# Working out the places of overflowing tokens inside the expert stage, and an output projection that begins with a prompt tile and ends with a sample tile in two column halves

## What is computed

```python
y = concat(gla_o, nsa_o) @ w_out                  # output projection, 1024 x 1024
x = x + gate1 * y                                  # residual; gate, scale, shift: one set for the
h2 = rmsnorm(x, g_ffn) * (1 + scale2) + shift2     # prompt, one for each sample sequence
top_logit, top_idx = top_k(h2 @ w_router + b_router, 4)   # of 32 experts
top_w = softmax(top_logit)
# tokens grouped by expert in blocks of 128 rows; for each block with its expert e:
gate = minimum(xb @ w_gate[e] + b_gate[e], 7)
up = clip(xb @ w_up[e] + b_up[e], -7, 7)
y[rows] += row_w * (((up + 1) * gate * sigmoid(1.702 * gate)) @ w_down[e] + b_down[e])
x = x + gate2 * y ; out = rmsnorm(x, g_final)
```

## Time and profile before

| | us |
|---|---|
| median of 3 runs | 1974.83 |
| lowest, highest | 1967.1, 1976.14 |
| the profiled execution: its own time | 1965.11 |
| its span, first to last instruction | 1963.4 |
| mean granted TensorE clock | 0.927 of full speed |
| TensorE, VectorE busy, of the span | 1737.5 (88%), 1436.0 (73%) |
| DMA over the span | 516.53 MB, mean 263 GB/s |

### The profile page before, as it was taken

How to read it: one execution, slowest core, us unless ns; L and a number is a source line. 1 busy time by engine, 2 the same in 40 slices (tenths; PEclk the granted TensorE clock), 3 DMA queues, 4 the chain that set the end, 5 groups by cost and what they waited for, 6 DMA issues and landing times. The chain is left out here.

```text
span 1963.4 us, 27138 instructions
## 1 busy us (share of the span) xinstructions
PE 1737.5 (88%) x9025; PEld 1347.3 (69%) x9025; DVE 1436.0 (73%) x1294; ACT 1094.1 (56%) x1031; POOL 298.8 (15%) x322
## 2 busy tenths in 40 slices
PE   4999857787775986899999999999999999999982
PEld 3767555554544445788888888888888888888872
DVE  4421164455453556799999999999999999999993
ACT  3211143444331223677777777777777777777762
POOL 0000032210010401121121211211212112121110
PEclk9999878778887986899999999999999999999996
DMA  9343264330024414899999999999999999999973
GB/s 356 129 165 133 70 191 130 125 113 1 1 66 151 156 73 181 332 362 371 368 365 378 368 370 367 367 378 361 375 376 360 380 371 370 377 367 370 379 260 114
DMA packets 112070, 516.53 MB, mean 263 GB/s; under 512 B 25853, under 2 KB 47117, under 8 KB 59242
## 3 DMA queue, kind: packets, MB, share of 16 engines
q1 hardware_dynamic: 99098, 485.77, 65.9%
q0 software_dynamic: 12912, 29.98, 5.6%
HBM read 502.69 MB, written 31.81 MB: 272 GB/s over the span
## 5 line engine op out<-in xcount | busy, mean ns | idle before, releaser
L2516 PE MATMUL banks<-split 128*128 128x512 f32 x4608 | 1081.9, 394 | 1.6 <-DVE split L2671 1.6
L2516 PEld LDWEIGHTS banks<-split 128*128 128x128 f32 x4608 | 863.4, 189 | 195.8 <-issue 14.7
L2671 DVE TENSOR_TENSOR split<-expert_buffers,split 128x2048 fp32r<-128x2048 f32 x384 | 867.5, 2285 | 63.2 <-ACT split L2606 61.2
L2606 ACT ACTIVATE split<-expert_buffers 128x2048 fp32r<-128x2048 f32 x384 | 733.3, 1918 | 251.4 <-PE banks L2516 225.4
L2454 POOL TENSOR_TENSOR expert_buffers<-routing 128x1 f32<-128x1 f32 x63 | 61.0, 968 | 912.4 <-PE banks L2523 531.0
L443 PE MATMUL banks<-w_in_high,hT_high 128*128 128x476 f32 (+1 forms) x240 | 93.4, 389 | 7.7 <-DVE hT_low L369 7.7
L382 DVE COPY arena<-banks 128x476 f32<-128x476 f32 (+1 forms) x15 | 9.8, 651 | 112.4 <-PE banks L443 112.4
L443 PE MATMUL banks<-w_in_low,hT_high 128*128 128x476 f32 (+1 forms) x240 | 91.8, 382 | 0.0
L443 PE MATMUL banks<-w_in_high,hT_low 128*128 128x476 f32 (+1 forms) x240 | 91.5, 381 | 0.0
L302 ACT ACTIVATE arena<-banks 128x476 f32<-128x476 f32 (+1 forms) x15 | 8.5, 566 | 126.6 <-PE banks L443 126.6
L2675 DVE TENSOR_TENSOR split<-banks,split 128x1024 fp32r<-128x1024 f32 x64 | 77.7, 1214 | 0.2 <-ACT split L2609 0.2
(11 more groups left out here) (347 smaller groups left out, 1721.6 us busy)
## 6 DMA issues: line engine op xcount, KB each, us to landing
expert_buffers<-in_w_gate SPq DMA_DIRECT2D x128, 1024.0 KB, 7.3
expert_buffers<-in_w_up SPq DMA_DIRECT2D x128, 1024.0 KB, 5.6
expert_buffers<-in_w_down SPq DMA_DIRECT2D x128, 1024.0 KB, 9.0
arena<-in_w_ada SPq DMA_DIRECT2D x16, 1024.0 KB, 4.8
w_in_landing<-in_w_in SPq DMA_DIRECT2D x6, 1904.0 KB, 15.0
arena<-in_w_ada SPq DMA_DIRECT2D x4, 2048.0 KB, 21.5
arena<-in_x_prompt SPq DMA_DIRECT2D x8, 512.0 KB, 10.4
arena<-in_cache_cmp POOLq DMA_DIRECT2D x32, 128.0 KB, 3.2
```

The lines of the kernel that those rows point to most:

```text
L2516: last = pe.matmul(ps[:, bank + c, :], x[:, kt * P:(kt + 1) * P].bitcast(F32R), wt.bitcast(F32R), start=False, stop=(kt == KT - 1 and x is ...
L2606: act.activation(high[:, j % RING_Q].bitcast(F32R), v, ACT.Copy).then_inc(s_high, 1)
L2671: dve.tensor_tensor(rest[:, j % RING_Q].bitcast(F32R), v, high[:, j % RING_Q], ALU.subtract).then_inc(s_rest, 1)
```

## The change

1. The nine instructions on overflowing tokens become a function `place_overflow`, which VectorE runs in the expert stage between `read_gate(0)` and the remainder of quarter 7. What it reads moves to memory that stays valid. `overflow` gets a wait on it (`s_over`).
2. `project_out(0)` starts once the first w_out half and tile 0 are there. The sample tile is turned behind it.
3. The sample tile's two matmuls for each `kt` write one bank: columns 0 to 511 to partitions 0 to 63, columns 512 to 1023 to partitions 64 to 127. ScalarE copies the upper half to partitions 0 to 63, VectorE multiplies each half by itself.
4. In the expert stage `used_blocks` moves: on SP, TensorE and ScalarE behind the first work. SP waits for one used quarter, not four, before it loads block 1's biases and weights. ScalarE rounds block 1's quarters 0 and 1 before it turns to that block's rows; VectorE takes quarter 0's remainder before reading up, quarter 1's before the activation.

```diff
@@ output_and_router, TensorE
-            for t, (t0, n) in enumerate(TILES):
+            def turn_mix(t):
+                n = TILES[t][1]
...
-            pe.wait_ge(s_mta, NT)
-            pe.wait_ge(s_mtd, NT)
+            for t in range(ST):
+                turn_mix(t)
             pe.wait_ge(s_wo, 16)
             def project_out(t):
                 t0, n = TILES[t]
+                pe.wait_ge(s_mta, t + 1)
+                pe.wait_ge(s_mtd, t + 1)
...
-                        last = pe.matmul(ps[0:n, 4 + 2 * (t % 2) + c, :], mixT[:, kt, t0:t0 + n],
-                                         wout[:, kt, c * 512:(c + 1) * 512], start=(kt == 0), stop=(kt == KT - 1))
+                        out = ps[0:n, 4 + 2 * (t % 2) + c, :] if t < ST else ps[64 * c:64 * c + 64, 4, :]
+                        last = pe.matmul(out, mixT[:, kt, t0:t0 + n], wout[:, kt, c * 512:(c + 1) * 512],
+                                         start=(kt == 0), stop=(kt == KT - 1))
...
             for t in range(NT):
                 project_out(t)
+                if t == 0:
+                    turn_mix(ST)
@@ output_and_router, ScalarE
+                if t == ST:
+                    act.wait_ge(s_yp, NT)
+                    act.activation(junk[0:n, 512:1024], ps[64:64 + n, 4, :], ACT.Copy).then_inc(s_upper, 1)
@@ output_and_router, VectorE
+                if who:
+                    dve.tensor_tensor(hh[:, 0:512], ps[0:n, 4, :], ex[0:n, who, 0, 0:512], ALU.mult)
+                    dve.wait_ge(s_upper, 1)
+                    link(dve.tensor_tensor(hh[:, 512:1024], junk[0:n, 512:1024], ex[0:n, who, 0, 512:1024], ALU.mult))
@@ experts, SP, step
-                    free = [4, 4, None]
+                    free = [1, 1, None]
@@ experts, TensorE
             turn_rows(0, first=True)
+            nb, nb1, nb2, _ = used_blocks(pe)
             gate(0, 0)
@@ experts, ScalarE
-            for j in range(1, 7):
+            for j in range(1, 6):
                 high_part(j, None)
+            nb, nb1, nb2, _ = used_blocks(act)
+            high_part(6, None)
             sigmoid(0)
             high_part(7, None)
+            for j in range(2):
+                high_part(j, 0)
             rows_T(1)
-            for j in range(4):
+            for j in range(2, 4):
                 high_part(j, 0)
@@ experts, VectorE
             read_gate(0, 4)
+            place_overflow(core, dve, linker(dve, s_dve, dve_count)).then_inc(s_over, 1)
             rest_part(7, None)
-            activations(0, 8)
+            rest_part(0, 0)
+            read_up(0, 8)
             rest_T(xh, xl, s_xh, 2, s_xt)
-            for j in range(4):
+            rest_part(1, 0)
+            activate(0)
+            for j in range(2, 4):
                 rest_part(j, 0)
```

More of the change, by code:

```diff
@@ L149, in take, with linker @@
         return self.tensor[:, at:at + words]
-def linker(engine, sem):
-    count = [0]
+def linker(engine, sem, count=None):
+    count = [0] if count is None else count
     def link(ins):
@@ L1905, in output_and_router @@
     core.tabf = late.take(NSLOT)
+    core.oh = oh = late.take(NT * TOPK * NE).rearrange("p (t j e) -> p t j e", t=NT, j=TOPK)
+    core.starts = late.take(NT * TOPK * NE).rearrange("p (t j e) -> p t j e", t=NT, j=TOPK)
+    core.wn, core.over, core.one4, core.first, core.oidx = (
+        late.take(NT * TOPK).rearrange("p (t j) -> p t j", t=NT) for _ in range(5))
+    core.ostart, core.token, core.slots = late.take(NE), late.take(NT), late.take(OVER)
+    wn, over, ostart = core.wn, core.over, core.ostart
     own.end = core.z_late
-    wt, wn = (own.take(NT * TOPK).rearrange("p (t j) -> p t j", t=NT) for _ in range(2))
+    wt = own.take(NT * TOPK).rearrange("p (t j) -> p t j", t=NT)
     wr = own.take(KT * NE).rearrange("p (k n) -> p k n", k=KT)
@@ L1919, in output_and_router @@
     nv0, wsum = own.take(NT), own.take(NT)
-    oh = own.take(NT * TOPK * NE).rearrange("p (t j e) -> p t j e", t=NT, j=TOPK)
     selb = own.take(NT * NE // 2).bitcast(BF16).rearrange("p (t e) -> p t e", t=NT)
     beforeb, onesb = own.take(P // 2).bitcast(BF16), own.take(P // 2).bitcast(BF16)
-    cnt, nover, oend, ostart, ones = (own.take(NE) for _ in range(5))
+    cnt, nover, oend, ones = (own.take(NE) for _ in range(4))
     pick = own.take(TOPK * NE).rearrange("p (j e) -> p j e", j=TOPK)
-    rank, over, one4, first, oidx = (own.take(NT * TOPK).rearrange("p (t j) -> p t j", t=NT) for _ in range(5))
+    rank = own.take(NT * TOPK).rearrange("p (t j) -> p t j", t=NT)
     low4, tok4, wt4 = (own.take(TOPK) for _ in range(3))
@@ L1931, in output_and_router @@
     at_exp = placed.take(NT * TOPK * 2 * NE).rearrange("p (t j w e) -> p t j w e", t=NT, j=TOPK, w=2)
-    starts = placed.take(NT * TOPK * NE).rearrange("p (t j e) -> p t j e", t=NT, j=TOPK)
     upper = Stack(core, core.z1 + NT * D, ARENA)
@@ L2101, in _ @@
                 project_out(t)
+                if t == 0:
+                    turn_mix(ST)
+                if t == 1:
+                    pe.wait_ge(s_mta, NT)
+                    pe.wait_ge(s_mtd, NT)
                 if t >= 1:
@@ L2164, in _ @@
             dve.tensor_copy(core.unit, core.const("one"))
-            for m in (rank, wn, oh):
+            dve.tensor_copy(core.token, core.const("token"))
+            dve.tensor_copy(core.slots, core.const("iota_k")[:, 0:OVER])
+            for m in (rank, wn, oh, over):
                 dve.memset(m, 0.0)
```

44 lines of the change are left out of this document (25 added, 19 removed).

## The result

| | before | changed |
|---|---|---|
| median, us (19 runs each) | 1970.72 | 1958.41 |
| lowest, highest | 1963.05, 1980.05 | 1951.04, 1968.27 |
| ratio, 95% interval | | 0.9935 [0.9917, 0.9953] |
| profiled execution: span, granted clock | 1963.4, 0.927 | 1959.3, 0.924 |

The change takes 12.3 us off; 1955.7 was forecast, in a range of 1946 to 1967. By the ratio it is 0.65% faster (0.47 to 0.83 by the interval), as the likeliest case had it. The steps did not come out as well as the sum.

The account below looks back on a forecast made before the run. TensorE was taken to bound the expert loop at 35.62 us a block, so the change only moves its start. 3.7 + 5.7 + 2.7 + 3.0 = 15.1 us off 1970.8 gave 1955.7, range 1946 to 1967.

Parts of the forecast that it names:

- the likeliest case: Whole kernel: faster by more than about 0.5%, chance 0.81.
- Step 1, tile 0 first: Output stage: projecting tile 0 before turning the sample tile brings tile 1's h2 3.7 us earlier.
- Step 2, the sample halves: Output stage: the sample tile's column halves run side by side, so VectorE begins that tile 5.7 us earlier.
- Step 3, the stage's end: End of output stage: without the nine overflow instructions the barrier opens 2.7 us earlier, GpSimd's drain last.
- Step 4, into the experts: First expert blocks: reordered loads and remainders gain 3.0 us, bounds a gain of 5 and a loss of 4.
- A, the port on tile 0: Output stage: GpSimd's bias split delays VectorE on tile 0; gain 13 us, time 1958, chance 0.14.
- B, halves not side by side: Sample tile's projection: still takes 14.2 us; gain 9.3 us, time 1961.5, chance 0.09.
- C: Experts' start: TensorE waits for quarter 7's remainder, the clock falls, 4 us lost; gain 8, time 1963, chance 0.07.
- D: Expert loop: another beat set by VectorE or DMA, slower; 1992 us at 1.2 us more a block, chance 0.03.

Follow-up runs that it names:

- busy_wait: The changed kernel with six more matmuls, result unused, on TensorE between tile 1's projection and turning tile 0's h2; 1957.03 us, ratio to before 0.9917.
- inputs_first: The changed kernel with prompt scales, g_ffn and tile 0's rows loaded ahead of the other tiles' rows; 1952.87 us, ratio to before 0.9922.
- no_tile0: The changed kernel with the sample tile turned before the projection starts, as before the change; 1961.54 us, ratio to before 0.9955.
- overflow_back: The changed kernel with the nine overflow instructions back at the end of the output stage; ratio to before 0.9934.
- sp_waits4: The changed kernel with SP again waiting for 4 used quarters, not 1, before loading block 1's biases; one execution, no ratio.
- gffn_early: The changed kernel with the load of g_ffn issued ahead of x, behind the router's weights; ratio to before 0.9936.

## Why the prediction came out as it did

**Step 1, tile 0 first: wrong.** Forecast 3.7 us at tile 1's h2; measured there, 2.2 us later than before (66.1, 63.9), and S is 0.4 us later (88.2, 87.8): 1.8 came back since tile 3's first half ran at full speed, a case that the forecast had named with 1.7. The start of the projection, the length of a tile and the place of the wait were as written. Two steps failed.

The first is "It was ready at 658.21 ... without the short wait for the projection it is ready at 657.9. TensorE turns it there: 5.6 us gained of 8.9, the rest turns into a wait for VectorE." VectorE was ready 42.7 us into the stage, not 40.2. g_ffn came 33.3 to 34.6 us into the stage in the five profiles with tile 0 first and the old order of loads, 29.6 to 32.1 in the four without; SP's issues of the rows, ahead of g_ffn's, took 8.3 to 8.7 us in them, not 7.1 to 8.2. Why they take longer was not tried and stays open. And the wait was priced at its length alone: behind 6.25 us of idleness TensorE's clock was 0.50 and 5.3 us of work were lost.

The second is "I leave GpSimd's start at 657". That is 39.4 into the stage; the split began at 43.2. By the forecast's own rule, VectorE is done 1.1 us behind GpSimd's second long operation, and this operation ended at 687.1, 62.8 into the stage, not 59.1. So tile 1's h2 was ready at 63.9, not at 60.2, and that alone takes all of the 3.7 us; the lower clock put TensorE another 2.2 behind it. busy_wait shows both: with the wait filled, h2(1) comes 1.9 us earlier than in the changed kernel, at 64.2, and waits there for VectorE. inputs_first, with the wait gone and the split off tile 1, has h2(1) 9.9 us earlier than before. The profiles show this cause; the times, as said, leave the step between nothing and some 6 us. (The cast's end in the forecast, 666.9, should by the same rule be 668.0; nothing hangs on it.)

**Step 2, the sample halves: right in size, the bound the other one.** Forecast 5.7 us, VectorE the bound; from S to VectorE's first half it is 9.2 us, before 14.35 (719.87 less 705.52): 5.1. TensorE arrives last, not VectorE: VectorE was free at 721.18, TensorE's second half ended at 721.57, and VectorE started 0.17 us behind it, as before (719.71, 719.87). The row names L2206, VectorE's own work, as the releaser, but that had been done for 0.56 us. TensorE's first half had taken 5.35 at a lower clock; in no_tile0, where it took 3.65, the two arrive within 0.1 us of each other. That weight loads of two halves over all rows might not hide was weighed ahead; the trace says 0.23 us a record with the weight loads beside them. The Trainium skill ("TensorE: Matmul & The Clock Gate", Part 3, What overlaps and what doesn't) has weight loads overlap with matmuls in flight only when the row group differs. This case's trace does not agree with it.

**Step 3, the stage's end: right as a size, less so as a gain.** From VectorE's start on the sample tile to E it is 37.9 us before and 35.2 after: 2.7, as forecast, with GpSimd's drain the last. overflow_back shows that the nine instructions themselves cost the experts' start 2.0 of it; the forecast had charged 1.1. The move is worth some half a microsecond.

**Step 4, into the experts: right in kind, too large.** The stall was 1.01 us (forecast 1.1), ScalarE's loads of block numbers did not show, gate(1) came straight behind the bias rows, and then waited 0.73 us for its third quarter, which the forecast had not. SP's earlier loads, which the forecast needed for it, are not shown to have mattered (sp_waits4). From E to B2, before and the two kernels with the old experts' stage have 80.5, 79.0 and 79.0, the nine with the new one but for overflow_back and sp_waits4 77.2 to 78.8, mean 77.6: 1.9 us, not 3.0. The 3.3 between the two profiles of before and after is partly scatter, of TensorE's time in block 0 for one.

**The sum.** -0.4 + 5.1 + 2.7 + 3.3 is 10.7 us, as at B2, and 12.3 was measured (9.3 to 16.4 by the interval). Forecast 15.1. The time is within 3 us of the forecast because three steps of four held about their size, and because the base that it was taken from, 1970.8 out of four executions, met the 1970.72 of nineteen; that was luck as much as care, since single executions of the kernel before lie 17 us apart.

**The rivals.** A, the port on tile 0, is real: it took tile 0 in five kernels, and h2(0) came 2.4 to 7.3 us later there than in the changed kernel in the four with the old order (45.3 to 50.2 against 42.9); the forecast let it begin with a split at 651, 33 us into the stage, and it was met with the split at 34 to 41. It is more likely than the 0.14 given. The Trainium skill ("SBUF — State Buffer", SBUF: two separate sides) says that a VectorE operation with two inputs in SBUF and a GpSimd operation that reads SBUF hold one pair of ports in turn, each for its whole length. The rows of gffn_early agree (3.57 and 6.89 us, each ending about 1.1 us behind GpSimd's). B, halves not side by side, did not come, nor did C (the stall came, the loss of 4 us did not) or D: the period is 35.62.

## What to carry to other kernels

A step that lets TensorE start sooner is worth something only if the operand of its next task comes sooner too; if not, price the wait at its length and then the lower clock behind it, here 5.3 us for a wait of 6.25. Look at the order of the loads before the order of the work: rows that nobody needed yet lay ahead of the scales on which the chain hung, and putting them behind brought h2(1) 12.1 us forward, where the first part had brought it back by 2. The profiles show this gain, the times do not yet (0.9922 against 0.9935). Long GpSimd operations with SBUF operands have to be put over a stretch in which the neighbouring VectorE work has more to spare than their full length.

## What the runs showed of the hardware that was not expected

A VectorE operation on almost nothing is held up beside a GpSimd operation like a large one: the cast of 128x4 numbers took 4.19 us in inputs_first, 0.17 in the tile before, while an operation that reads PSUM beside SBUF kept its time: L2278 in gffn_early, 1.21 us from 671.06, next to GpSimd's cast that ran from 670.11 to 673.73. And behind a wait of 6.25 us TensorE's clock was at 1.2 GHz (0.50 over 10 us), behind one of 1.81 us only for a part of the time (0.88 over 14 us).
